# Value products with the values stationary, no drain of attention behind the projections, and the output product ended tile by tile, in a hybrid decoder layer

## What is computed

```python
z = x @ W_in                                     # split by columns into q_a, k_a, v_a, indexer, q_m, k_m, v_m, o_m, gates
# group A: 8 heads of 64, sparse attention
score[t,s] = sum_h w[t,h] * relu(q_idx[t,h] . k_idx[s])       # each query keeps its top 128 causal keys
y_a = softmax(q.k/8 - slope_h*(t-s), over the kept keys) @ v_a
# group B: 4 mLSTM heads of 128 (causal conv and silu on q and k, decay matrix from the gates,
#          normalised by max(|den|, exp(-m)), norm over the head, times sigmoid(o_m))
mix = concat(y_a, y_m) @ W_out
x1  = LN(alpha*x + mix)
# hierarchical experts: 4 groups x 8 experts of width 256; the best group, in it the two best experts
ffn = sum over the token's two experts of weight * (silu(x1 @ gate_e) * (x1 @ up_e)) @ down_e
x2  = LN(alpha*x1 + ffn)
out = x2 + sigmoid(x2 @ W_g) * (p @ W_p)         # p: 512 x 256
```

## Time and profile before

| | |
|---|---|
| median of three runs | 721.0 us |
| the profiled execution | 722.4 us |
| its span | 720.6 us |
| TensorE busy | 648.5 us (90%), 3,782 products |
| VectorE busy | 348.8 us (48%) |
| ScalarE busy | 178.9 us (25%) |
| POOL busy | 168.3 us (23%) |
| mean granted TensorE clock | 0.957 |
| DMA | 151.21 MB, mean 210 GB/s |

### The profile page before, as it was taken

The page is one execution under the profiler, slowest core; times in us unless marked ns, Lnnn a source line. Parts: engine busy times, 40 slices in busy tenths (PEclk is TensorE's granted clock), DMA queues, the critical chain, the costliest instruction groups (busy, mean ns, idle before and its releaser), DMA issues.

```text
span 720.6 us, 10045 instructions
## 1 busy us (share of the span) xinstructions
PE 648.5 (90%) x3782; PEld 454.1 (63%) x3782; DVE 348.8 (48%) x803; ACT 178.9 (25%) x344; POOL 168.3 (23%) x175
## 2 busy tenths in 40 slices
PE   4999999999999999799626999999999997868997
PEld 3768887878787787688523555555555553423785
DVE  3379998657564576616762112211111111117846
ACT  5165132324323233410210111111111111024311
POOL 7206414001010000351103233333333332110100
PEclk9959999989999999999876999999999999998999
DMA  6402301203100500077296888999999999987003
GB/s 239 189 1 89 146 30 61 115 0 115 62 1 0 234 1 0 1 264 300 95 399 250 280 321 297 410 415 417 414 414 414 414 414 416 419 333 302 3 0 117
DMA packets 30438, 151.21 MB, mean 210 GB/s; under 512 B 7308, under 2 KB 7564, under 8 KB 16432
## 3 DMA queue, kind: packets, MB, share of 16 engines
q1 hardware_dynamic: 23984, 142.08, 49.9%
q0 software_dynamic: 6400, 8.42, 3.3%
HBM read 148.36 MB, written 14.68 MB: 226 GB/s over the span
## 4 chain that ended last, share of the span: by engine, by line
PE 64%; DMA 6%; SPq 5%; DVE 5%; issue 2%; ACT 1%; DVEq 0%; POOLq 0%; ACTq 0%
PE bank L1890 15%; PE bank L1599 9%; PE bank L1600 8%; PE bank L1601 8%; PE bank L1905 8%; SPq L449 5%; DMA raw<-in_w_exp_dram 4%; PE bank L1679 3%; PE bank L1954 2%; PE bank L1700 2%; PE bank L1880 2%; PE bank L1688 2%; PE bank L1729 1%; PE bank L1897 1%; PE bank L1720 1%
## 5 line engine op out<-in xcount | busy, mean ns | idle before, releaser
L1514 DVE COPY rows_x<-bank 128x128 f32<-128x128 f32 x40 | 11.6, 291 | 195.1 <-PE bank L1897 195.1
L1599 PE MATMUL bank<-w_hi,a_hi 128*128 128x384 f32 (+1 forms) x240 | 88.0, 367 | 5.9 <-POOL w_lo L578 2.9
L1601 PE MATMUL bank<-w_hi,a_lo 128*128 128x384 f32 (+1 forms) x240 | 86.5, 361 | 0.0
L1600 PE MATMUL bank<-w_lo,a_hi 128*128 128x384 f32 (+1 forms) x240 | 86.4, 360 | 0.0
L1599 PE MATMUL bank<-a_hi,w_hi 128*128 128x512 f32 (+1 forms) x176 | 71.1, 404 | 11.3 <-POOL w_lo L571 9.9
L666 POOL DMA_INDIRECT pair_dram<-rows_x,row_put x40 | 40.5, 1013 | 166.4 <-ACT rows_x L908 166.4
L1890 PE MATMUL bank<-raw,rows_x 128*64 128x256 f32 x544 | 65.6, 393 | 6.6 <-DMA raw<-in_w_exp_dram 5.0
L1600 PE MATMUL bank<-a_lo,w_hi 128*128 128x512 f32 (+1 forms) x176 | 69.5, 395 | 0.0
L1601 PE MATMUL bank<-a_hi,w_lo 128*128 128x512 f32 (+1 forms) x176 | 69.2, 393 | 0.0
L1890 PEld LDWEIGHTS bank<-raw,rows_x 128*64 128x64 f32 x544 | 40.2, 142 | 36.0 <-issue 14.7
L1890 PE MATMUL bank<-slots,rows_x 128*64 128x256 f32 x512 | 58.5, 380 | 3.2 <-DMA slots<-in_w_exp_dram 3.2
(11 more groups left out here) (250 smaller groups left out, 1032.6 us busy)
## 6 DMA issues: line engine op xcount, KB each, us to landing
raw<-in_w_exp_dram SPq DMA_DIRECT2D x42, 1024.0 KB, 13.1
slots<-in_w_exp_dram SPq DMA_DIRECT2D x36, 1024.0 KB, 12.1
rows_x<-in_w_exp_dram SPq DMA_DIRECT2D x12, 1024.0 KB, 13.9
raw<-in_w_in_dram SPq DMA_DIRECT2D x19, 512.0 KB, 4.0
raw<-in_w_wide_dram SPq DMA_DIRECT2D x4, 1536.0 KB, 6.8
y<-in_w_exp_dram SPq DMA_DIRECT2D x6, 1024.0 KB, 14.8
raw<-in_w_out_dram SPq DMA_DIRECT2D x4, 1024.0 KB, 9.2
raw<-pair_dram SPq DMA_DIRECT2D x4, 1024.0 KB, 9.1
```

The costliest lines, as they stand in the source:

```text
L1599: t_.matmul(o, lh, rh, start=first, stop=False)
L1600: t_.matmul(o, lh, rl, start=False, stop=False)
L1601: return t_.matmul(o, ll, rh, start=False, stop=last)
```

## The change

- `pv` makes the values stationary and the probabilities moving: a product is 64 x 128, the two heads of a pair on the two halves of the columns of the array, and the result stands transposed in the bank, head by token. `attn_out` becomes a copy, and the four blocks of attention need no `turn_y`. All of a pair's `pv` stand in stages 4 and 5; the transposed probabilities of the first head are kept in `prob_t0`.
- The probabilities are divided by their sums before they are transposed: `normalise` on VectorE, one reciprocal and two scalings a stage; `turn` waits for it (`s_norm`).
- `ATTEND` goes from 12, 18, 24, 30 to 12, 17, 22, 26.
- Behind the last projection stand two `turn_y`, the last numerator and the output product. Its quarters come in another order, the low parts of its first are awaited block by block, and the two quarters of the mLSTM are made tile by tile, with the transposes of tiles 0 to 2 between them. On VectorE `norm_tiles` is written out in another order.
- SP loads pT and ple_proj with the router's weights, the weights of experts 2 and 3 between the stores, and ln2's behind the first load of the ring.
- Three of the eight embedding products move ahead (`AHEAD = 3`): two behind the logits, one in the tables. The first tokens are transposed ahead of the tables of the rest.
- The end: SP's waits for the last items stand behind its branch, the pair rows come as eight DMAs of 512 KB, and a gate product waits for half of the low parts.

The diff, cut to its core:

```diff
-ATTEND = [12, 18, 24, 30]
+ATTEND = [12, 17, 22, 26]
...
-OUT_Q = [0, 2, 1, 3]
-TURNS = [0, 4, 1, 5, 2, 6, 3, 7]
+OUT_Q = [2, 0, 1, 3]
+TURNS = [0, 1, 2, 3, 5, 4, 6, 7]
+def y_columns(k):
+    return y_a[:, k, :] if k < NG else (proj_bank + lstm_bank)[0 if k == 6 else k - NG][:, :]
...
     for q in range(4):
+        if q == 3:
+            sp.wait_ge(s_pv, NT * NG)
...
-    sp.wait_ge(s_yt, NK)
+    sp.wait_ge(s_yt, HM)
     sp.dma_start(wr_raw, d["w_router"]).then_inc(s_wr, 16)
+    sp.dma_start(p_raw, d["pT"]).then_inc(s_pr, 16)
+    sp.dma_start(proj_raw, d["ple_proj"]).then_inc(s_pw, 16)
...
     for t in range(NT):
-        sp.dma_start(pair_of(t), pair_dram.rearrange("(k t p) c -> t p k c", k=2, p=P)[t, :, :, :])\
-            .then_inc(s_pair[t], 16)
+        for k in range(2):
+            r = (k * NT + t) * P
+            sp.dma_start(pair_of(t)[:, k, :], pair_dram[r:r + P, :]).then_inc((s_pair, s_xn)[k][t], 16)
...
+    def normalise(g, j):
+        hh, b = 2 * j // NT, 2 * j % NT
+        dve.wait_ge(s_exp, 8 * g + 2 * j + 2)
+        v.reciprocal(row_inv[:, b:b + 2, hh:hh + 1], row_sums[g % 2][:, b:b + 2, hh:hh + 1]).then_inc(s_yinv, 1)
+        dve.wait_ge(s_yinv, 4 * g + j + 1)
+        for e in range(2):
+            part = prob[:, e, 0:(b + e + 1) * P]
+            v.tensor_scalar(part, part, row_inv[:, b + e, hh:hh + 1], None, ALU.mult).then_inc(s_norm, 1)
...
-        v.tensor_copy(prob_t[:, U % 2, 0:n], turn_bank[:, 0:n]).then_inc(s_probt, 1)
+        if hh and b >= 2:
+            dve.wait_ge(s_pv, NT * g + b - 1)
+        elif g:
+            dve.wait_ge(s_pv, NT * (g - 1) + b + 1 + 2 * hh)
+        v.tensor_copy(turned(u), turn_bank[:, 0:(b + 1) * P]).then_inc(s_probt, 1)
...
+        v.tensor_copy(y_a[:, g, :], attn_bank[:, :]).then_inc(s_ya, 1)
...
     def attention(g, j):
+        if 1 <= j <= 4:
+            normalise(g, j - 1)
...
+    for i in range(NG):
+        y_low(i)
+    lstm_variance(HM - 1)
+    for i in range(NG, 2 * NG - 1):
+        y_low(i)
+    lstm_out(HM - 1)
+    y_low(2 * NG - 1)
...
+    mixed(0, 0)
+    mixed(0, 1)
+    dve.wait_ge(s_lnw, 32)
+    norm_centre(0, s_ln)
+    norm_scale(0, s_ln, s_rs)
+    mixed(1, 0)
+    mixed(1, 1)
+    norm_centre(1, s_ln)
+    norm_scale(1, s_ln, s_rs)
+    low_first(0)
     dve.wait_ge(s_wrs, 1)
     v.tensor_tensor(w_lo[:, WR_AT:3 * GW], wr_raw.rearrange("p k c -> p (k c)"),
                     w_hi[:, WR_AT:3 * GW].bitcast(F32), ALU.subtract).then_inc(s_wrs, 1)
-    def mixed(t):
-        dve.wait_ge(s_xn[t], 16)
-        for half in range(2):
-            dve.wait_ge(s_wot, 2 * t + half + 1)
-            residual(t, half)
-            dve.wait_ge(s_r, 2 * t + half + 1)
-            norm_stats(t, half, s_bn)
-        norm_variance(t, s_bn, 3 * t + 2, s_ve)
-    norm_tiles(mixed, s_rs, s_ln, s_lnw, turned_1, s_x1hi, s_x1lo)
+    mixed(2, 0)
+    mixed(2, 1)
+    norm_centre(2, s_ln)
+    mixed(3, 0)
+    norm_scale(2, s_ln, s_rs)
+    low_first(1)
+    mixed(3, 1)
+    norm_centre(3, s_ln)
+    low_first(2)
+    norm_scale(3, s_ln, s_rs)
+    low_first(3)
...
     for t in range(NT):
-        expert_sum(t)
+        expert_sum(t, 0)
         if t:
             turned_low(2 * t - 2, turned_2, s_x2hi, s_x2lo)
             turned_low(2 * t - 1, turned_2, s_x2hi, s_x2lo)
+        expert_sum(t, 1)
         expert_variance(t)
         if t == 0:
             dve.wait_ge(s_lnw2, 32)
-        norm_apply(t, s_ln2, s_rs2)
+        norm_centre(t, s_ln2)
+        norm_scale(t, s_ln2, s_rs2)
...
     def turn(g, u):
         U, b = 8 * g + u, u % NT
-        pe.wait_ge(s_exp, U + 1)
+        pe.wait_ge(s_norm, U + 1)
...
-    def pv(g, u):
-        U, hh, b = 8 * g + u, u // NT, u % NT
-        pe.wait_ge(s_probt, U + 1)
-        if u == 0:
-            pe.wait_ge(s_evac, step_no(g, STEPS - 1) + 1)
-            if g:
-                pe.wait_ge(s_ya, g)
-        o = attn_bank[:, (2 * b + hh) * DA:(2 * b + hh + 1) * DA]
+    def pv(g, b):
+        pe.wait_ge(s_probt, 8 * g + NT + b + 1)
+        pe.wait_ge(s_evac, step_no(g, TALL + b) + 1)
+        if b == 0 and g:
+            pe.wait_ge(s_ya, g)
         for s in range(b + 1):
-            mm = t_.matmul(o, prob_t[:, U % 2, s * P:(s + 1) * P], v_a[:, g % 2, s, hh * DA:(hh + 1) * DA],
-                           start=s == 0, stop=s == b)
+            for hh in range(2):
+                rows = slice(hh * DA, (hh + 1) * DA)
+                mm = t_.matmul(attn_bank[rows, b * P:(b + 1) * P], v_a[:, g % 2, s, rows],
+                               turned(hh * NT + b)[:, s * P:(s + 1) * P], start=s == 0, stop=s == b)
         mm.then_inc(s_pv, 1)
...
-            if 2 <= j <= 5:
-                pv(g, 2 * j - 4 + e)
+            if 4 <= j <= 5:
+                pv(g, 2 * j - 8 + e)
...
-    for j in range(NG):
-        work(NG, j)
-        turn_y(2 * j)
-        if j < 3:
-            turn_y(2 * j + 1)
+    pe.wait_ge(s_evac, NSTEP - 1)
+    turn_y(4)
+    work(NG, 0)
+    pe.wait_ge(s_evac, NSTEP)
+    turn_y(5)
...
+    pe.wait_ge(s_masked, 8 * NG)
+    pe.wait_ge(s_olo, 1)
+    token_major(2, 2, 0)
+    pe.wait_ge(s_ylo, 6)
+    turn_y(6)
+    token_major(2, 3, 0)
+    token_major(2, 1, 0)
     pe.wait_ge(s_ylo, 7)
+    token_major(2, 0, 0).then_inc(s_wo, 1)
+    pe.wait_ge(s_olo, 2)
     pe.wait_ge(s_hid, 2 * NG)
-    pe.wait_ge(s_olo, 1)
-    for t in range(NT):
-        mm = token_major(0, t, 0)
-    mm.then_inc(s_wo, 1)
-    pe.wait_ge(s_olo, 2)
-    token_major(2, 0, 1)
-    token_major(2, 2, 1)
+    def mlstm_part(t):
+        pe.wait_ge(s_olo, 3)
+        token_major(1, t, 2).then_inc(s_wot, 1)
+        pe.wait_ge(s_olo, 4)
+        token_major(3, t, 3).then_inc(s_wot, 1)
+    token_major(0, 0, 1)
+    token_major(0, 1, 1)
     turn_y(7)
-    token_major(2, 3, 1)
+    token_major(0, 2, 1)
     pe.wait_ge(s_ylo, NK)
-    token_major(2, 1, 1).then_inc(s_wo, 1)
-    pe.wait_ge(s_olo, 3)
-    for t in range(NT):
-        token_major(1, t, 2).then_inc(s_wot, 1)
-        if t == 0:
-            pe.wait_ge(s_olo, 4)
-        token_major(3, t, 3).then_inc(s_wot, 1)
+    mlstm_part(0)
+    token_major(0, 3, 1).then_inc(s_wo, 1)
+    mlstm_part(1)
...
+    def embed(u):
+        t, half = u // 2, u % 2
+        weights = proj_raw.rearrange("p (u c) -> p u c", u=4)
+        for k in range(2):
+            mm = t_.matmul(ple_bank[u][:, :], p_raw[:, k, t * P:(t + 1) * P], weights[:, 2 * half + k, :],
+                           start=k == 0, stop=k == 1)
+        mm.then_inc(s_pp, 1)
...
+    token_major(1, 2, 2).then_inc(s_wot, 1)
+    turn_first(0)
+    token_major(3, 2, 3).then_inc(s_wot, 1)
+    token_major(1, 3, 2).then_inc(s_wot, 1)
+    turn_first(1)
+    token_major(3, 3, 3).then_inc(s_wot, 1)
+    turn_first(2)
+    pe.wait_ge(s_wrs, 2)
+    route(0)
+    pe.wait_ge(s_pr, 16)
+    pe.wait_ge(s_pw, 16)
+    embed(0)
+    turn_first(3)
     turn_logits(0)
     route(1)
     turn_logits(1)
+    embed(1)
...
             tables(4, FIXED)
+            pe.wait_ge(s_pev, 1)
+            embed(2)
+            turn_tokens(0, 0)
             tables(TB_FIXED + 3, NE)
-            turn_tokens(0, 0)
+            pe.wait_ge(s_pev, AHEAD)
...
+        if half == 0:
+            pe.wait_ge(s_x2lo, 2 * t + 1 + q)
         if q % 2 == 0:
-            pe.wait_ge(s_x2lo, 2 * t + 2)
```

213 lines of the change are left out of this document (110 added, 103 removed).

## The result

The changed kernel takes 718.4 us (median of 17 runs, 713.15 to 723.54), the kernel before 722.8 us on the same chips (17 runs, 719.7 to 727.89). The ratio is 0.994, with a 95% interval from 0.9921 to 0.9959: 4.4 us less by the medians, where I had forecast 10.5. The time lies inside the stated range, by less than 1 us. The direction was right and the size was not: less than half of it came.

A forecast was written before the change was run, and what follows sets the result against it. TensorE was taken as the bound, idle for long only in two stages on chains through other engines. Terms -1.0 - 2.9 - 2.9 - 3.5 = -10.3 us gave 712.1 profiled, 710.5 median; range 697 to 719.

The forecast's parts named there:

- Behind the last projection: From the last projection to the first output product: 22.7 us fall to 5.4, saving 17.3.
- The loop: Attention inside the projection loop: 1.5 us more attention work, 12.4 more stalls behind VectorE's scalings, 2.4 for mode-change drains.
- my walk: Step-by-step estimate of TensorE's waits for VectorE's scalings in the projection loop: 16.2 us of stalls, 3.8 before.
- Output product to logits: From the first output product to the logits: 64.4 us to 61.4, saving 2.9, with seventh transposes 1.9 us late.
- First tokens: Gather of the first tokens ahead of the experts: with an empty queue, 6.88 us fall to 4.0, saving 2.9.
- Experts: The experts' stage: nothing changes inside, its start and end move together.
- End: Behind the last expert product: first gate product comes earlier, saving 3.5 us (1 to 5).
- rival 1: Projection loop: VectorE has room, so the 12.4 us of stalls fall to 2; 700 us, down to 697; chance 0.27.
- rival 2: Attention: value products do not overlap, or every group drains twice; price 8.6 us, 717 to 719; chance 0.09.
- rival 3: Projection loop: stalls bring down TensorE's clock, 2.8 us a fall, 17 in all; 727 us; chance 0.06.
- rival 4: Experts: DMA ends them at its own time, so earlier gains are lost; price 6.9 us, 717; chance 0.05.
- my three signs of being wrong: Loop stalls under 8 us, clock under 0.95 there, or a longer experts' stage would show the forecast wrong.

The follow-up runs named there:

- a4: The changed kernel without the reciprocals and scalings that divide the probabilities by their sums: 708.2 us, ratio 0.9785 to the kernel before.
- a3: The changed kernel with POOL's power ahead of its subtraction for W_out (`split_out(1)`): 712.7 us, ratio 0.9852 to the kernel before.
- a2: The changed kernel with low parts moved ahead of the last head's variance on VectorE: 709.2 us, ratio 0.9795 to the kernel before.
- the first profile: The first profiled execution of the changed kernel, nothing altered: 722.0 us, span 720.2 us.
- the control: The changed kernel run again unaltered and profiled a second time: 718.6 us, ratio 0.9933 to the kernel before; profile span 712.7 us.
- d1: a2 with the inverse and both scalings of the probabilities moved from VectorE to POOL: 706.2 us, ratio 0.9766 to the kernel before.
- d3: d2 with two embedding products ahead instead of three: 705.2 us, ratio 0.9752 to the kernel before.
- b4: The changed kernel with stores and ln2's loads ordered as before; profile only: 5.9 us from the gather's issue to the first expert product.
- b3: The changed kernel with pair rows again in four DMAs of 1 MB; profile only: first gate product 21.6 us behind the last down product.
- c2: c1 with the scalings also at the very start of a step on VectorE: 710.6 us, ratio 0.9814 to the kernel before.
- b2: a2 with the scalings at the end of the same step on VectorE, not the start of the next: 710.7 us, ratio 0.9829 to before.
- c1: a2 with the variance of heads 0 and 1 one step later, and head outputs moved later too: 712.7 us, ratio 0.985 to before.
- d2: a2 with the inverse moved from VectorE to POOL and the scalings to ScalarE: 704.7 us, ratio 0.9745 to the kernel before.

## Why the forecast was off

**Behind the last projection: right.** Forecast 5.4 us, measured 5.3.

**The loop: right in sum by luck, not in its parts.** The last projection was to end at 295.2 and ended at 295.9. The stalls were over-sized: 16.2 us in my walk, 12.3 in the trace. One reason is the scaling itself: I took 0.54 us for 512 columns from the convolution's row, and a scaling of 384 and one of 512 together take 0.82, so the division of a head pair takes 3.5 us of VectorE and not 4.1. (The walk's own items, seven named and nine of 0.4 to 0.8, come to 16.6 at the least.) What was missing is the clock: slow projections cost 4.7 us where before one cost 2.1, and against a4, whose loop is at full clock throughout, all of TensorE's work took 7.2 us longer, of which some 3 were there before. The term that I put at nothing cost 4 us, and the stalls came out 4 us short of the walk. A head pair's value products take 3.1 us, in three groups of 0.44, 0.99 and 1.68, where I had 2.1 and 0.6 for the mode change.

**Output product to logits: the step that failed.** This is the term that was mis-sized. I wrote that the seventh transposes are "1.9 us late". I had seen the low part behind the variance and behind `round_out(1)`, but priced the variance at its 2.7 us alone, and never asked what POOL does meanwhile. The wait was 5.26 us, 3.7 of it POOL's hold (a3), and a clock fall of 1.6 us stood behind it. So the term was 1.9 us and should have been 6.9; without the wait (a2) the stage takes 60.3 us, 6.9 less than in the control and 1.1 less than forecast. Another 1.4 of the first profile are in its second logits (4.4 us from 365.1, 3.0 in the control); d1 to d3 have no such wait and show those too (4.5), so they do not come from it. The whole row is 7.6 us too small by the first profile and 5.8 by the control; the whole miss is 6.1. (In the recorded sums 61.0 became 61.4 without a reason, and 712.1 less 1.4 is 710.7, not 710.5; neither matters here.)

**First tokens: right** (2.9 us forecast, 3.3 measured; the gather takes 3.50 where I took 4.0). Little of it is the order of the stores and of ln2's loads (b4).

**Experts: right**, 258.8 us for 258.7.

**End: right to the first gate product** (20.6 forecast, 19.8 measured; up to 1.5 of it by the smaller loads, b3). What I left out is behind it. With three embedding products gone from here TensorE is through before the second norm, and behind the gap its products run at half clock in some executions: 2.9 us more in the first profile, nothing in the control.

**The rivals.** VectorE does not have room (rival 1): that needed its division off it. The value products overlap (rival 2 fell). The clock (rival 3) was the right mechanism with the wrong price: I had 17 us from five falls on, and there were four slow projections of 0.6 to 1.4 us. The experts' stage kept its length (258.8 us), so what is gained ahead of it arrives behind it (rival 4 fell).

**The signs.** None of my three signs of being wrong came: gaps of 12.3 us, a clock of 0.96, experts as long as before. All three looked at the loop and the experts, and none at the stage where the term was wrong.

## What to carry to other kernels

When work moves to an engine's queue, write down for the waits that end there not only what stands ahead in that queue but what the neighbour that can hold the engine runs in the same microseconds. When a moved operation does not gain, look for the hold behind it as well as for the stall ahead of it: in c2 it had only found another victim. Here moving work about within VectorE's full queue moved the stall (b2, c1), and taking the division to another engine took it away (d1, d2). And filler work in the gap of an engine that is finished early cost nothing here, and kept the products behind it at full clock in three profiles of three; a gain in the medians was not seen.
